# Two-layer block: split products in the forgetting attention, and the lo half of a weight chunk stored over its raw form

## The reference, cut to what matters

```python
F = cumsum(log_sigmoid(f_logit + b_forget), axis=1)       # (L, H)
s = einsum('bhqk', q, k) * 64 ** -0.5 + F[t] - F[s]       # per head
s = where(s_pos <= t_pos, s, -inf)
y = softmax(s) @ v
```

## Time and profile before

| what | value |
|---|---|
| median of 3 runs | 2390.04 us |
| profiled execution | 2395.49 us, span 2393.8 us |
| PE busy | 2243.4 us, 94% |
| DVE busy | 1019.3 us, 43% |
| ACT busy | 712.7 us, 30% |
| POOL busy | 620.3 us, 26% |
| mean granted clock of TensorE | 0.91 |
| read from HBM | 257.88 MB |

### The profile page before, as it was taken

The page is one execution under the profiler, slowest core; times in us unless marked ns, Lnnn a source line. Parts: engine busy times, 40 slices in busy tenths (PEclk is TensorE's granted clock), DMA queues, the critical chain, the costliest instruction groups (busy, mean ns, idle before and its releaser), DMA issues.

```text
span 2393.8 us, 29247 instructions
## 1 busy us (share of the span) xinstructions
PE 2243.4 (94%) x11946; PEld 1857.1 (78%) x11946; DVE 1019.3 (43%) x1621; ACT 712.7 (30%) x909; POOL 620.3 (26%) x147
## 2 busy tenths in 40 slices
PE   6999985999997999979999997999999988999997
PEld 6698874888766666669999997887578776888886
DVE  4699764423327566542322235302442324332224
ACT  2422232322225545431111123323342223122121
POOL 0334300234310000024433331231004332434430
PEclk6999985799998999989999996898569997999998
DMA  8455400132214999732222221121003321232210
GB/s 245 135 179 183 137 18 1 36 106 88 70 36 141 337 341 342 279 106 89 88 90 92 98 88 36 54 88 54 0 1 107 105 71 53 89 104 88 94 64 36
DMA packets 176219, 261.30 MB, mean 109 GB/s; under 512 B 13209, under 2 KB 141898, under 8 KB 176126
## 3 DMA queue, kind: packets, MB, share of 16 engines
q1 hardware_dynamic: 175550, 258.96, 32.2%
q10 hardware_dynamic: 576, 1.05, 0.1%
HBM read 257.88 MB, written 2.11 MB: 109 GB/s over the span
## 4 chain that ended last, share of the span: by engine, by line
PE 82%; DVE 14%; issue 1%; ACT 1%; DMA 1%; SPq 0%; DVEq 0%; ACTq 0%
PE PS L690 56%; PE PS L1109 6%; PE PS L1131 4%; PE PS L924 3%; DVE macc L1760 2%; PE PS L1223 2%; PE PS L746 1%; DVE Hf L1731 1%; DVE sc L1875 1%; DVE max L1874 1%; PE PS L915 1%; DVE macc L1758 1%; DVE Hf L1712 1%; PE PS L890 1%; PE PS L840 1%
## 5 line engine op out<-in xcount | busy, mean ns | idle before, releaser
L652 POOL TENSOR_TENSOR w_lo<-w_raw,w_hi 128x2048 fp32r<-128x2048 f32 x133 | 617.9, 4648 | 1689.6 <-ACT w_hi L1313 1689.6
L690 PE MATMUL PS<-HH,w_hi 128*128 128x512 f32 (+1 forms) x1936 | 598.2, 347 | 25.2 <-DVE HL L1705 25.2
L690 PE MATMUL PS<-HL,w_hi 128*128 128x512 f32 (+1 forms) x1936 | 598.7, 347 | 0.0
L690 PE MATMUL PS<-HH,w_lo 128*128 128x512 f32 (+1 forms) x1936 | 596.3, 346 | 0.0
L1313 ACT ACTIVATE w_hi<-w_raw 128x2048 fp32r<-128x2048 f32 x133 | 254.3, 1913 | 534.0 <-PE PS L690 491.9
L690 PEld LDWEIGHTS PS<-HH,w_hi 128*128 128x128 f32 x1936 | 339.2, 191 | 74.8 <-issue 28.0
L690 PEld LDWEIGHTS PS<-HL,w_hi 128*128 128x128 f32 x1936 | 338.5, 190 | 45.5
L690 PEld LDWEIGHTS PS<-HH,w_lo 128*128 128x128 f32 x1936 | 338.1, 190 | 45.0
L2278 DVE TENSOR_TENSOR actf<-PS,sg 128x528 f32<-128x528 f32 (+1 forms) x44 | 30.8, 700 | 421.0 <-PE PS L690 421.0
L2289 DVE TENSOR_TENSOR yacc<-yacc,PS 128x528 f32<-128x528 f32 (+1 forms) x176 | 122.4, 695 | 105.7 <-PE PS L690 105.7
L2171 DVE TENSOR_TENSOR m_lo<-m_raw,m_hi 128x2048 fp32r<-128x2048 f32 x56 | 128.1, 2292 | 77.3 <-ACT m_hi L1520 76.8
(11 more groups left out here) (356 smaller groups left out, 2878.8 us busy)
## 6 DMA issues: line engine op xcount, KB each, us to landing
w_raw<-in_w_in SPq DMA_DIRECT2D x49, 1024.0 KB, 5.1
w_raw<-in_w_ffn_in SPq DMA_DIRECT2D x44, 1024.0 KB, 4.9
m_raw<-in_w_exp_gate SPq DMA_DIRECT2D x56, 512.0 KB, 4.3
m_raw<-in_w_exp_up SPq DMA_DIRECT2D x56, 512.0 KB, 5.5
m_raw<-in_w_exp_down SPq DMA_DIRECT2D x56, 512.0 KB, 4.8
w_raw<-in_w_ffn_out SPq DMA_DIRECT2D x22, 1024.0 KB, 4.8
mod_raw<-in_w_mod SPq DMA_DIRECT2D x20, 1024.0 KB, 5.0
w_raw<-in_w_out SPq DMA_DIRECT2D x8, 1024.0 KB, 5.0
```

The source lines that it names most:

```text
L652: pool.tensor_tensor(w_lo[:, s, :], w_raw[:, s, :], w_hi[:, s, :].bitcast(F32), ALU.subtract).then_inc(split, 1)
L690: ins = mm(o, l, r, **k)
```

## The change

It has two parts.

**Weight chunks.** `w_lo` takes the addresses of `w_raw`: GpSimd writes its difference over the raw chunk. A load may thus start only when TensorE is done with the chunk three before it, and waits on `begun` in place of `split`. The 24 KB that this frees hold a fourth buffer of the experts' weights (which had lain in the ring's area) and the new tiles of the attention.

```diff
-        w_raw = at("w_raw", B, [RING, CH]); B += RING * CH * 4
+        w_raw = at("w_raw", B, [RING, CH])
+        w_lo = at("w_lo", B, [RING, CH], F32R); B += RING * CH * 4
         w_hi = at("w_hi", B, [RING, CH], F32R); B += RING * CH * 4
-        w_lo = at("w_lo", B, [RING, CH], F32R); B += RING * CH * 4
...
                 if c >= RING:
-                    sp.wait_ge(split, c - RING + 1 + more)
+                    sp.wait_ge(begun, c - RING + 2 + more)
```

```diff
-                if n_p == SPREAD_AT:
-                    pe.wait_ge(negF_ready, 1)
-                    for h in range(8):
-                        s = W.claim()
-                        for b, (x0, n) in enumerate(halves(TALL)):
-                            ins = mm(PS[:, s, b, 0:n], ident[0:8, h:h + 1].to_broadcast([8, P]), negF[0:8, x0:x0 + n],
-                                     start=True, stop=True)
-                        W.made(ins)
...
+            def fox_logits(m, i):
...
+                for n, (q_, k_) in enumerate(((qh, kh), (qh, kl), (ql, kh), (None, None))):
+                    for cs in cols:
+                        for e in range(2):
+                            hp = slice(64 * e, 64 * e + 64)
+                            if n < 3:
+                                mm(outs[e][:, cs], q_[hp, m, rows], k_[hp, m, cs], start=n == 0, stop=False, skip_group_check=True)
+                            else:
+                                h = 2 * m + e
+                                mm(outs[e][:, cs], selF[hp, h:h + 1].to_broadcast([64, P]), FS[hp, cs], start=False, stop=False,
+                                   skip_group_check=True)
...
+                        ins = mm(outs[e][:, c0:cs.stop], identR[:, :], outR[:, c0 - d0:cs.stop - d0], start=False, stop=True,
+                                 skip_group_check=True)
...
+            def fox_values(x):
...
+                W.wait_released(tgroup[x])
+                s = W.claim()
...
+                        for n, (l, r) in enumerate(((vh, ph_), (vl, ph_), (vh, pl_))):
+                            ins = mm(o[:, q0:256], l[kp, j, vs], r, start=j == 4 and n == 0, stop=j == 2 * hf_ + 1 and n == 2,
+                                     skip_group_check=True)
...
+            for n in range(len(FOX) + 4):
+                if n < len(FOX):
+                    fox_logits(*FOX[n])
+                if 0 <= n - 2 < len(FOX):
+                    fox_transposes(n - 2)
+                if 0 <= n - 4 < len(FOX) and FOX[n - 4][1] % 2 == 1:
+                    fox_values(n - 4)
```

ScalarE's order in a step is exponential of n, hi copy of the transposes of n-2, output of n-4. VectorE's is:

```diff
+            for n in range(len(FOX) + 4):
+                if n < len(FOX):
+                    fox_max(n)
+                if 0 <= n - 1 < len(FOX):
+                    fox_scale(n - 1)
...
+                if 0 <= n - 3 < len(FOX):
+                    fox_lo(n - 3, t_at[n - 3])
```

More of the change, by code:

```diff
@@ L1227, in _ @@
-            combos2 = [(i, h) for i in range(NTOK) for h in range(8)]
-            W.wait_released(W.g - 1)
[L1229 to L1234, removed]
+                rows = slice(P * i, P * i + P)
@@ new lines, in fox_logits @@
+                d0 = META + P * i
+                last = []
+                for e in range(2):
+                    for cs in cols:
+                        c0 = max(cs.start, d0)
+                        ins = mm(outs[e][:, c0:cs.stop], identR[:, :], outR[:, c0 - d0:cs.stop - d0], start=False, stop=True,
+                                 skip_group_check=True)
+                    if i == NTOK - 1:
+                        W.made(ins)
+                if i < NTOK - 1:
+                    W.made(ins)
@@ L1642, in _ @@
                 W.skip(2)
-            for h in range(8):
-                s = W.arrive()
-                W.release(af(sv(Hf[:, h, :], TALL), ps(s, TALL), ACT.Copy))
             for _ in range(2):
@@ new lines, in _, with fox_exp @@
+                    W.skip(1)
+                    af(vh[0:n, t, c0:c0 + 256], PS[0:n, s, 0, 0:256], ACT.Copy).then_inc(kqv_hi, 1)
+            def fox_exp(x):
+                m, i = FOX[x]
+                n_all = META + P * (i + 1)
+                act.wait_ge(max_ready, x + 1)
+                for e in range(2):
+                    if e == 0 or i == NTOK - 1:
+                        s = W.arrive()
+                    src = PS[:, s, e, 0:n_all] if i < NTOK - 1 else PS[:, s, :, :].rearrange("p b n -> p (b n)")[:, 0:n_all]
+                    c = 2 * x + e
+                    ins = af(pr2[:, x % 3, e, 0:n_all], src, ACT.Exp, bias=nmax[:, c:c + 1], scale=0.125, accum_out=den[:, c:c + 1])
+                    if e == 1 or i == NTOK - 1:
+                        W.release(ins)
@@ L2326, in _ @@
             W.skip(1)
+            L.mark(ts(FS[:, :], ones[:, 0:1].to_broadcast([P, TALL]), 0.0, None, ALU.mult))
+            L.mark(ts(selF[:, :], ones[:, 0:8], 0.0, None, ALU.mult))
+            L.mark(v_.tensor_copy(identR[:, :], ident[:, :]))
+            L.mark(v_.tensor_copy(outR[:, :], outside[:, :]))
+            L.wait()
+            for b in range(4):
+                L.mark(v_.tensor_copy(selF[32 * b:32 * b + 8, :], ident[32 * b:32 * b + 8, 32 * b:32 * b + 8]))
             dve.wait_ge(gla_act, 2 + seq + 1 + 1)
@@ L2363, in _ @@
[L2363 to L2366 removed]
+                dve.wait_ge(kqv_hi, kqv)
+                W.release(tt(sv(kl[:, m, :], TALL), ps(s, TALL), sv(kh[:, m, :].bitcast(F32), TALL), ALU.subtract))
+            for m in range(4):
+                kqv += 1
+                s = W.arrive()
+                dve.wait_ge(kqv_hi, kqv)
+                W.release(tt(ql[:, m, :], ps(s), qh[:, m, :].bitcast(F32), ALU.subtract))
@@ new lines, in _, with fox_max @@
+            for c0 in (0, 256):
+                for t in range(5):
+                    n = P if t < 4 else META
+                    kqv += 1
+                    s = W.arrive()
+                    dve.wait_ge(kqv_hi, kqv)
+                    W.release(tt(vl[0:n, t, c0:c0 + 256], PS[0:n, s, 0, 0:256], vh[0:n, t, c0:c0 + 256].bitcast(F32), ALU.subtract))
+            logit_groups, fox_parts = {}, {"n": 0}
+            def fox_max(x):
+                m, i = FOX[x]
+                n_all = META + P * (i + 1)
+                top = nmax[:, 2 * x:2 * x + 2]
+                if i < NTOK - 1:
+                    s = W.arrive()
+                    W.skip(1)
+                    L(v_.tensor_reduce(top.unsqueeze(2), PS[:, s, :, 0:n_all], AX, ALU.max))
+                else:
+                    for e in range(2):
+                        s = W.arrive()
+                        W.skip(1)
+                        L(v_.tensor_reduce(top[:, e:e + 1], PS[:, s, :, :].rearrange("p b n -> p (b n)")[:, 0:n_all], AX, ALU.max))
+                logit_groups[x] = W.g - 1
+                ts(top, top, -0.125, None, ALU.mult).then_inc(max_ready, 1)
@@ new lines, in _ @@
+            t_at = {}
+            for n in range(len(FOX) + 4):
+                if n < len(FOX):
+                    fox_max(n)
+                if 0 <= n - 1 < len(FOX):
+                    fox_scale(n - 1)
+                if 0 <= n - 2 < len(FOX):
+                    t_at[n - 2] = W.g
+                    W.skip(1 if FOX[n - 2][1] < NTOK - 1 else 2)
+                if 0 <= n - 3 < len(FOX):
+                    fox_lo(n - 3, t_at[n - 3])
+                if 0 <= n - 4 < len(FOX) and FOX[n - 4][1] % 2 == 1:
+                    W.skip(1)
```

183 lines of the change are left out of this document (135 added, 48 removed).

## The result

The changed kernel takes **2444.68 us** (median of 4 runs, 2441.54 to 2447.55), the kernel before 2390.45 us on the same chip: ratio **1.0225** (95% interval 1.0207 to 1.0243), 54 us slower. The traced execution took 2443.95 us, span 2442.1, which is 48.3 more than the span before. The traced execution of before lay 5 us above its median, the one of after at its own; this is the difference between 48 and 54. Timed once more (experiment 10), the ratio was 1.0179 (1.0150 to 1.0207).

The account below looks back on a forecast made before the run. Took the kernel as TensorE-bound (82% of the chain), with three places where the change works. Terms +68 - 14 + 0.5 - 20 + 2.5 = +37 us, so 2427 us on the median's scale; range 2404 to 2462.

Parts of the forecast that it names:

- Part 1, the loads: First projection: modulation loads queue behind the waiting chunk load; 4.9 us per period, 14 times, +68 us, bounds 62 to 74.
- the prediction's list: First projection, one period from chunk begin T: load issues, landings, hi and lo, products, sums; next chunk at T+16.6.
- the bound that I had given and not taken: First projection: 74 us of loss if TensorE's sums run at the lower clock and hops add up.
- Part 4, behind it: Both merges' held-up adds and the chunk behind the last modulation tile at low clock: together +2.5 us.
- Part 2, the spread: Second projection, fifth chunk: sixteen K=8 products (11.7 us) go, and 2.7 us of lowered clock: -14 us.
- Part 3, the attention: Forgetting attention: head pairs by four query blocks, 110 us taken between ends 94 and 142, from 130.3: -20 us.
- rival 2: Attention gains nothing: lower clock, four passes for narrow products, 142 us; total 2459 us; chance 0.17.
- my two ends: Forgetting attention's length: 115 us at the lower clock, 94 us at the full one.
- the 12 that I had worked out for it: Attention: some 50 tiling-mode changes at 0.24 us each would add some 12 us, left inside the range.
- 3 (not held up): First projection: products not held up by GpSimd, +1.4 us a period, 20 us; total 2363 or 2379; chance 0.06.
- 4 (half the loss): First projection's loads cost half, so gain and loss cancel: total 2385 to 2400 us; chance 0.04.

Follow-up runs that it names:

- experiment 10: The changed kernel, unchanged, timed and traced a second time beside the kernel before: 2440.55 us, ratio 1.0179.
- Experiment 1: Changed kernel with the modulation loads moved two chunks earlier in SyncE's list: 2365.58 us, ratio 0.9882.
- experiments 2 and 3: Kernel before with only lo over raw and the load's wait on `begun`: 2474.46 us; the same with modulation loads moved ahead: 2400.90 us.
- experiment 4: Changed kernel, late load order kept, GpSimd's first-projection subtraction held until VectorE finished the modulation tile: 2391.93 us, ratio 0.9992.
- experiments 2, 3 and 9: experiments 2 and 3, and the kernel before, unchanged, traced a second time: 2402.11 us, 1.0026 against its own other runs.

## Why the prediction was right, point by point

Forecast 2427 us, measured 2444.7; the sign, the place and the mechanism of the loss were right. The sum was 18 us short. 11 us of that are in the terms, as below: the spans differ by 48.3 where I had 37. The other 6 are the step from one execution to the median: I took off 5.5 us because the traced execution of before lay that far above its median, and the traced one of the changed kernel lay 0.7 below its own.

**Part 1, the loads** (+68, bounds 62 to 74; measured +73.5). The period in the chain above follows the prediction's list from T = 207.00: chunk issued at T+0.37 (0.3), modulation 0.41 later, landed at T+8.2 (8.5), first product over at T+12.3 (12.2), next chunk at T+16.6 (16.6). The mean of 16.9 is longer since some transfers take 8.5 to 8.7 us, and since in some periods TensorE's sums run at the lower clock and take 1.01 us in place of 0.61, the bound that I had given and not taken. Experiment 1 shows the cause, experiments 2 and 3 that the first part of the change alone carries the loss, and experiment 4 the share of GpSimd.

**Part 4, behind it** (+2.5 for all; measured 7.4 up to the second projection in the first pair of traces). I had priced one chunk behind the last modulation tile at the low clock. The chain behind that tile:

```profile
343.80 13.01 PE PS L704 x96
...
368.76 4.40 issue
```

The chunk took 13.01 instead of 11.46 us, less than priced; the 4.40 us before the gated MLP's products, 2.51 before, are put down to nothing by the profile. But the program has TensorE wait there for VectorE's last operation on `v`, and VectorE's timeline ends 0.1 us before TensorE starts again at 373.16:

```profile
363.65 6.87 DVE L1960 TENSOR_TENSOR v<-v,ln_rows 128x512 f32<-128x512 f32 x4
370.56 2.50 DVE L1963 TENSOR_TENSOR v<-v,ln_rows 128x512 f32<-128x512 f32 x4
```

One of the first four takes 5.06 us, from 365.47, beside a subtraction of GpSimd's from 364.99 to 369.97. The same group was held up before as well (one of 4.98 us), but began 7 us ahead of TensorE's last product and not 5. The rest lies in the gated MLP's and attention stages before the merge, where the offset grows to 79 us, and 2 us in the experts' stage, which differed by up to 5 us among kernels that are alike there. How much of the 7.4 us is the change's is not settled by one pair: from the last sums to the first merge's first add the two traces of before take 203.4 and 206.0 us, the three with the changed kernel's first layer 209.0, 208.5 and 207.0, which is 3.5 us in the mean and close to the term. The merge's add was held up, 3.6 us where it has 0.69 else, but that is nothing new, and here the prediction was wrong: in the kernel before the same add took 4.1 to 4.6 us. From the attention's end on the two traces differ by 0.5 us.

**Part 2, the spread** (-14; measured -15.1, and +15.8 put back). Right. Of the 15.8, 1.7 are a wait for a slot that the kernel before did not have inside its spread.

**Part 3, the attention** (-20, ends 94 and 142; measured -18.0, a length of 112.8 where I took 110). The length was forecast well, the gain partly by luck: 6.8 of the 18.0 us come with the ring and not with the new attention, by a clock that comes back earlier, which I had not foreseen (experiments 2, 3 and 9). Each disputed point can be read. Two heads' K=64 products do run together, and a narrow product costs one pass (TensorE's timeline, x2 are the two heads; start, length, what):

```profile
1753.97 0.31 PE L1292 MATMUL PS<-PT1h,vl 128*64 128x128 f32 x1
1754.07 0.31 PE L1292 MATMUL PS<-PT1l,vh 128*64 128x128 f32 x1
1754.31 0.49 PE L1243 MATMUL PS<-kh,qh 64*128 64x144 f32 x2
1754.60 0.41 PE L1243 MATMUL PS<-kl,qh 64*128 64x144 f32 x2
1754.81 0.41 PE L1243 MATMUL PS<-kh,ql 64*128 64x144 f32 x2
```

Products of 128 columns start 0.107 us apart at the lower clock, and the two heads' products of 144 columns take 0.21 us together. Pairs of 144 are thus no cheaper than two products, but those of 400 columns follow each other every 0.33 us, the time of one head's columns at 1.2 GHz. So rival 2's four passes were out. The waits were priced at 7.7 us per pair, 25 in all, and are 20.9. The chain shows one link for link as the prediction built it, maximum, scaling, lo halves, next products:

```profile
1760.66 0.73 DVE nmax L2501
...
1761.90 0.29 DVE pr L2518
1762.19 0.87 DVE PT1l L2532
1763.06 0.33 DVE PMl L2534
...
1763.53 4.00 PE PS L1292 x18
```

What I had too low is TensorE's own work. By my two ends, 115 at 0.50 and 94 at 1.00, and in proportion to the clock's period between them, a mean clock of 0.62 would have given about 107 us. (Two slips are in that working: the values come to 9.0 us and not 9.2, and the end at the full clock does not take off the 6 us at the start, so it would be 88. With both put right it would have been about 104.) The values take 6.56 + 4.00 = 10.6 us per pair at the lower clock instead of 9.2, and each block's mask 0.64 us, over 2.5 per pair instead of 1.1, since its end is waited for. As for the Trainium skill's drain at a change of tiling mode (TensorEngine Tiling (Array Packing), Key Properties): in the timeline above the step from 64 output columns back to 64 rows is 0.24 us where its neighbours are 0.107, so 0.13, and the next step is 0.29 where the one behind it is 0.21. If both belong to the change, as they come with it, that is some 0.2 us, and some 50 changes make 10 us (an estimate). That is a part of what I missed, and near the 12 that I had worked out for it and not put in the sum.

Of the rivals, 3 (not held up) and 4 (half the loss) are refuted by the 4.06 us of the first product. Rival 2's total of 2459 was nearer to the measured time than 2427 was, about 14 us off against 18, but for none of its reasons: the attention gained.

## What to carry to other kernels

An in-order queue of loads turns one load's wait into a wait of all loads behind it. When the condition of a wait is made later, look at what stands behind it in the list, not only whether that load itself is still in time; here rearranged loads were worth 70 to 80 us, and left no loss of the cheaper buffer that these runs can tell from drift. Where an engine frees slots that the bound engine wants, let it do the freeing step first and the step that opens new work afterwards: one moved step gave 31 us. The best kernel of this study has both, 2333.7 us, 2.6% faster than the kernel before.

## What the runs showed of the hardware

- A VectorE product of 128x256 elements that meets GpSimd's subtraction of 2048 columns waits for its end: 4.1 us instead of 0.35, with one operand or with two. Row maxima and replacements run beside it at their own 0.56 and 0.55 us.
- The attention's busy time fell from 89.9 to 72.8 us with the same matmuls, only because another engine's order changed: the granted clock went from 0.62 to 0.81. The change of clock was worth 17 us here, the shorter waits 14; what links the two is not shown.
- Fp32r products cost by their columns, 0.107 us at 128 and 0.213 at 256 at the lower clock. Two products on different 64-row halves of the array with 128 output columns run together: a pair of 400 columns takes 0.33 us, the time of one, a pair of 144 columns 0.21.
- Kernels that are the same up to a point reach it at times that differ by up to 6 us in 1480, and once by 12. Compared from event to event, the first projection's periods, the second projection and the attention repeat within 1.5 us; the first 105 us differed by up to 8.6 us and the experts' stage by up to 5.
